# Attention probabilities divided by their sum on ScalarE before their transposes, instead of a division behind the value products

## The reference, cut to what matters

```python
def sink_probs(scores, mask, sinks):
    sc = jnp.where(mask, scores, NEG_INF)
    m = jnp.maximum(jnp.max(sc, axis=-1, keepdims=True), sink)
    p = jnp.exp(sc - m)
    denom = jnp.sum(p, axis=-1, keepdims=True) + jnp.exp(sink - m)
    return p / denom

def attn_prompt(q, k, v, sinks):   # blocks of 128 queries, each with its own and the previous 128 keys
    ...
    p = sink_probs(scores, mask, sinks)
    o = jnp.einsum("bnkgqs,bnskd->bnqkgd", p, vv)
```

## Time and profile before

| | |
|---|---|
| median of 3 runs | 907.57 us (906.25 to 912.13) |
| the profiled execution's own time | 907.48 us |
| its span in the profile | 905.5 us |
| mean granted TensorE clock | 0.996 |
| PE busy | 874.9 us, 97% of the span, 5635 instructions |
| PEld busy | 781.9 us (86%) |
| DVE busy | 558.0 us (62%) |
| ACT busy | 401.1 us (44%) |
| POOL busy | 253.1 us (28%) |

### The profile page before, as it was taken

How to read it: one execution, slowest core, us unless ns; L and a number is a source line. 1 busy time by engine, 2 the same in 40 slices (tenths; PEclk the granted TensorE clock), 3 DMA queues, 4 the chain that set the end, 5 groups by cost and what they waited for, 6 DMA issues and landing times. The chain is left out here.

```text
span 905.5 us, 16890 instructions
## 1 busy us (share of the span) xinstructions
PE 874.9 (97%) x5635; PEld 781.9 (86%) x5636; DVE 558.0 (62%) x1025; ACT 401.1 (44%) x732; POOL 253.1 (28%) x250
## 2 busy tenths in 40 slices
PE   8999999999999999999999999999799999999995
PEld 7777776878999999999999999999778888888884
DVE  5677775543489655665434955445887758487661
ACT  5666665311254443333211212223527757577562
POOL 2434332344231000000002540000152455364562
PEclk9999999999999999999999999999999999999998
DMA  8433331350532432223973138862549988989933
GB/s 281 140 96 115 127 76 36 99 215 1 193 97 74 147 107 96 95 96 110 335 282 90 65 91 285 303 222 93 170 135 312 338 269 292 335 247 315 299 43 60
DMA packets 79552, 153.55 MB, mean 170 GB/s; under 512 B 10701, under 2 KB 44173, under 8 KB 78960
## 3 DMA queue, kind: packets, MB, share of 16 engines
q1 hardware_dynamic: 72000, 134.84, 43.3%
q0 software_dynamic: 7488, 17.85, 8.6%
HBM read 122.80 MB, written 40.30 MB: 180 GB/s over the span
## 5 line engine op out<-in xcount | busy, mean ns | idle before, releaser
L1492 POOL TENSOR_TENSOR hT_lo_raw<-hT_lo_raw,arena 128x1056 f32<-128x1056 f32 x7 | 23.3, 3326 | 227.2 <-DVE arena L1738 227.2
L2486 DVE TENSOR_TENSOR hT_lo<-room,hT_hi (+1 forms) x32 | 72.2, 2292 | 17.2 <-ACT hT_hi L2175 17.2
L79 PE MATMUL psum<-w_hi,hT_hi 128*128 128x512 f32 (+3 forms) x216 | 79.1, 366 | 1.7 <-DVE hT_lo L1111 1.0
L79 PE MATMUL psum<-hT_hi,x_xT_hi 128*128 (+1 forms) x192 | 77.8, 405 | 1.4 <-DVE x_xT_lo L2638 0.7
L80 PE MATMUL psum<-hT_lo,x_xT_hi 128*128 (+1 forms) x192 | 75.7, 394 | 0.0
L81 PE MATMUL psum<-hT_hi,x_xT_lo 128*128 (+1 forms) x192 | 75.7, 394 | 0.0
L81 PE MATMUL psum<-w_hi,hT_lo 128*128 128x512 f32 (+3 forms) x216 | 75.3, 349 | 0.0
L80 PE MATMUL psum<-w_lo,hT_hi 128*128 128x512 f32 (+3 forms) x216 | 75.1, 348 | 0.0
L2115 POOL DMA_INDIRECT out_y<-y,put_at x23 | 46.1, 2005 | 91.1 <-DMA out_y<-y,put_at 67.8
L2175 ACT ACTIVATE hT_hi<-room (+1 forms) x32 | 59.9, 1922 | 11.5 <-PE psum L81 10.1
L1532 ACT ACTIVATE arena<-arena 128x264 f32<-128x264 f32 x64 | 26.9, 425 | 76.2 <-DVE arena L1727 75.6
(11 more groups left out here) (414 smaller groups left out, 2626.2 us busy)
## 6 DMA issues: line engine op xcount, KB each, us to landing
room<-in_w_gu SPq DMA_DIRECT2D x16, 2048.0 KB, 11.4
dn_raw<-in_w_dn SPq DMA_DIRECT2D x16, 1024.0 KB, 7.4
arena<-in_w_ab SPq DMA_DIRECT2D x24, 512.0 KB, 4.5
gate_rows<-arena SPq DMA_DIRECT2D x32, 264.0 KB, 2.4
arena<-gate_rows SPq DMA_DIRECT2D x16, 528.0 KB, 4.0
xT_chunk<-in_xT SPq DMA_DIRECT2D x8, 528.0 KB, 4.0
x_in<-in_x SPq DMA_DIRECT2D x8, 512.0 KB, 5.5
h_rows<-h_raw SPq DMA_DIRECT2D x8, 512.0 KB, 4.1
```

What stands on the lines that cost most here:

```text
L79: eng.matmul(out, lh, rh, start=first and k == 0, stop=False)
L1492: pool.tensor_tensor(here, here, part[v % 2], ALU.add).then_inc(h2_summed, 1)
L2486: dve.tensor_tensor(gu_lo[:, buf, ks], gu_raw[:, buf, ks], gu_hi[:, buf, ks].bitcast(F32), ALU.subtract).then_inc(gu_lo_made.sem, 1)
```

## The change

Each half's probabilities are now multiplied by the reciprocal of their own sum on ACT, in place, before they are transposed (`scale_probs`: four activations of 128x256 with a per-row scale). DVE inverts the sums half by half (`invert_dens(t, gp)`: two small operations). `dens_turn`, the spread to 128x512, `copy_rT` and `o_scale` are gone; `oa_high` and `oa_low` read bank 5 directly. Both copies of turned probabilities are DVE's. `oa_low` and the first inversion stand ahead of the second `mask_scores` on DVE; on ACT the first `probs` stands ahead of `copy_kv`, and the second `scale_probs` behind `h_high`. `mix(3)` goes between the two halves of `v_product(5)`. In the dense phase `low(4)` goes ahead of `weight_sum(0, "S4")`.

```diff
             def probs(t, gp):
                 if t >= 1:
-                    act.wait_ge(rd_made, t)
+                    act.wait_ge(rd_made, u - 1)
-            def copy_second_pT(t):
-                ...
-            def copy_rT(t):
-                ...
+            def scale_probs(t, gp):
+                k0 = block_keys(t)
+                act.wait_ge(rd_made, 2 * t + gp + 1)
+                for kv, i, j, g in heads_of(gp):
+                    ins = act.activation(p_sb[:, gp, j, k0:], p_sb[:, gp, j, k0:], ACT.Copy, scale=rden[:, gp, j:j + 1])
+                ins.then_inc(p_scaled, 1)
             def oa_high(t):
                 if t < PT:
-                    act.wait_ge(o_scaled, t + 1)
-                    src = o_n
+                    act.wait_ge(o_made, 2 * t + 2)
+                    src = bank(psum, 5)
 # ACT, step s = PT (the last)
                     probs(done, 0)
+                    scale_probs(done, 0)
+                    probs(done, 1)
                     copy_q(s)
-                    probs(done, 1)
+                    scale_probs(done, 1)
                     copy_kv(s)
-                    copy_second_pT(done)
                     vs_high(0)
-                    copy_rT(done)
 # ACT, steps s = 1 to 7
                     if s > 0:
+                        probs(done, 0)
                         copy_kv(s)
-                        probs(done, 0)
+                        scale_probs(done, 0)
                         probs(done, 1)
                     h_high(s + 1)
                     if s > 0:
-                        copy_second_pT(done)
+                        scale_probs(done, 1)
                     ...
                         copy_q(s)
                         copy_qT(s)
-                    if s > 0:
-                        copy_rT(done)
+                        oa_high(done)
 # PE
             def project_q(t, k0, k1):
-                if t >= 2:
-                    pe.wait_ge(rT_copied, t - 1)
             def probs_turn(t, gp):
-                pe.wait_ge(p_made, u + 1)
+                pe.wait_ge(p_scaled, u + 1)
             def values(t, gp):
                 if t >= 1:
-                    pe.wait_ge(o_scaled, t)
+                    pe.wait_ge(oa_lo_made, t)
-            def dens_turn(t):
-                ...
                 qk_turn(s)
-                dens_turn(s - 1)
             mix(2)
-            mix(3)
             for i in range(5, NT):
                 for half in range(2):
                     v_product(i, half)
+                    if i == 5 and half == 0:
+                        mix(3)
                 mix(i - 1)
 # DVE
-            def invert_dens(t):
-                ...
-            def o_scale(t):
-                ...
+            def invert_dens(t, gp):
+                dve.wait_ge(p_made, 2 * t + gp + 1)
+                step.did(dve.tensor_tensor(rden[:, gp, :], den[:, gp, :], sink_e[:, gp, :], ALU.add))
+                dve.reciprocal(rden[:, gp, :], rden[:, gp, :]).then_inc(rd_made, 1)
                 mask_scores(done, 0)
                 if s + 1 < NT:
                     h_scale(s + 1)
+                if done >= 1:
+                    oa_low(done - 1)
+                invert_dens(done, 0)
                 mask_scores(done, 1)
                 ...
                 copy_pT(done, 0)
+                invert_dens(done, 1)
                 ...
                     k_scale(s)
-                if done >= 1:
-                    oa_low(done - 1)
-                invert_dens(done)
+                copy_pT(done, 1)
                 ...
-                o_scale(done)
 # DVE, dense phase
             for piece in range(2):
                 fourth_sum(piece)
+            low(SLOTS - 1)
             weight_sum(0, "S4")
             dve.wait_ge(ob_lo, US)
             ...
-                low(g + SLOTS - 1)
+                if g > 0:
+                    low(g + SLOTS - 1)
```

More of the change, by code:

```diff
@@ L165, in attention_phase @@
         s_sb, p_sb = sp_sb[:, 0], sp_sb[:, 1:]
-        rT, o_n = (sp_sb[:, 0, 2 * n:2 * n + 2, :].rearrange("p g c -> p (g c)") for n in range(2))
         z, _ = brief((("z_qkv", [P, AW + KVW]), ("behind_z", [P, G * KV * HD])))
@@ L248, in attention_phase @@
         pT_made, pT_copied = sem("pT_made"), sem("pT_copied")
-        o_made, o_scaled = sem("o_made"), sem("o_scaled")
-        rd_made, rT_made, rT_copied = sem("rd_made"), sem("rT_made"), sem("rT_copied")
+        o_made, rd_made, p_scaled = sem("o_made"), sem("rd_made"), sem("p_scaled")
         oT_made, oa_hi_made, oa_lo_made = sem("oT_made"), sem("oa_hi_made"), sem("oa_lo_made")
@@ L639, in _ @@
                         copy_qT(s)
-                    if s > 0:
-                        copy_rT(done)
+                        oa_high(done)
                     if s + 3 < NT:
                         square(s + 3)
-                if s > 0:
+                if s == PT:
                     oa_high(done)
@@ L842, in sample_values @@
                 pe.wait_ge(v_cache_in, DMA)
-                pe.wait_ge(o_scaled, PT)
+                pe.wait_ge(oa_lo_made, PT)
                 d = slice(kv * HD, (kv + 1) * HD)
@@ L875, in sample_v_sum @@
                 pe.wait_ge(z_copied, 2 * NT)
-                pe.wait_ge(rT_copied, PT)
                 pe.matmul(bank(psum, 0)[0:NS, :], groups_sum, hs_parts, start=True, stop=True).then_inc(v_made, 1)
@@ L943, in _ @@
             values(PT - 1, 1)
-            dens_turn(PT - 1)
             qk_turn(PT)
@@ L1076, in copy_pT @@
                                 psum[:, 6 + first:8, :].rearrange("p a c -> p (a c)")).then_inc(pT_copied, 1)
-            def invert_dens(t):
[L1079 to L1086, removed]
-            def o_scale(t):
-                dve.wait_ge(o_made, 2 * t + 2)
-                dve.wait_ge(rT_copied, t + 1)
-                dve.tensor_tensor(o_n, bank(psum, 5), rT, ALU.mult).then_inc(o_scaled, 1)
+            def invert_dens(t, gp):
+                dve.wait_ge(p_made, 2 * t + gp + 1)
+                step.did(dve.tensor_tensor(rden[:, gp, :], den[:, gp, :], sink_e[:, gp, :], ALU.add))
+                dve.reciprocal(rden[:, gp, :], rden[:, gp, :]).then_inc(rd_made, 1)
             def oa_low(t):
                 dve.wait_ge(oa_hi_made, t + 1)
-                src = o_n if t < PT else bank(psum, 4)
+                src = bank(psum, 5 if t < PT else 4)
                 dve.tensor_tensor(oaT[1][:, :, toks(t)],
```

## The result

| | before | after |
|---|---|---|
| median of runs, us | 907.9 (906.25 to 913.83, 6 runs) | 931.34 (929.4 to 932.63, 6 runs) |
| ratio, 95% interval | | 1.0252 [1.0228, 1.0277] |
| profiled execution, own time / span, us | 907.48 / 905.5 | 932.39 / 930.4 |
| mean granted clock of TensorE | 0.996 | 0.989 |
| PE busy, share of the span | 97% | 94% |

The prediction was 924.4 (917 to 932): the sign, the place and the chain are as forecast, the sum is 7 us short. The page after opens with

A forecast was written before the change was run, and what follows sets the result against it. PE, busy 97% of the span, was taken to bound the kernel, so only its work or waits count. From 907.5, attention +19.2, `mix(3)` -1.7 and the gate -0.6 gave 924.4 us, range 917 to 932.

The forecast's parts named there:

- the second turn: Attention step, PE's transpose of the second half's probabilities: starts at 14.25 instead of 11.49 behind the scores, 2.75 us later.
- q's road: Attention, q's way through ACT and DVE from the second turn to the next scores: sets 5.07 us, unchanged.
- the second Exps: Attention step, ACT's Exps of the second half: start at 9.4 instead of 8.31, behind the later second mask.
- the stands: Attention step, PE's waits for ACT's scaling: 0.7 us before the first turn, about 2.05 before the second.
- The scaling: Attention, ACT's four passes for a half: 0.40 us apart and 0.49 for the last, 1.69 us in all.
- the cheap bound: Attention, scaling passes only 0.26 us apart, 1.2 us a half; the sum would be 3 to 4 us smaller.
- `h_high` in between: Attention, ACT's `h_high` moved between the second Exps and the second scaling: adds 1.05 us to the chain.
- `dens_turn` in the shade: Attention, PE's turn of denominators (0.4 to 0.6 us) stands in the shade of q's road; dropping it gives nothing back.
- Exclusion of GpSimd and DVE: Attention, `h_low` on GpSimd could delay the second inversion, holding the scaling 0.6 us in 6 steps: +3.6, upper end only.
- Step 8, mix, gate: Sample tile +0.9 us; `mix(3)` loses its whole wait, -1.7; the gate's wait moves to g = 5, -0.6.
- Attention: +19.2 us: Whole attention: 16.5 us for steps 1 to 6, 1.8 for step 7, 0.9 for step 8; uncertainty +-3.5.
- rival (d): Attention, PE's clock falls: 2.5 us behind each second turn at 1.2 GHz, 7 steps, 18 us more: 942; 6%.

The follow-up runs named there:

- measured with one: Changed kernel with only one head of four scaled in each half, division of the other three left out: 918.27 us, ratio 1.0116.
- the turns back: Changed kernel with the four transposes of the dropped denominators' turn put back on PE, result not read: 929.7 us, ratio 1.025.
- The two moves alone: Kernel before with only `mix(3)` between the halves of `v_product(5)` and `low(4)` ahead of the sum: 904.71 us, ratio 0.9975.
- the filled kernel: Changed kernel with 8 useless 128-column products on PE ahead of the second turn, steps 2 to 8: 926.81 us, ratio 1.0215.
- q's last part ahead: Changed kernel with the last part of q's projection ahead of the second turn instead of behind it: 919.39 us, ratio 1.013.
- the two filled kernels: Changed kernel with useless PE products ahead of the second turn: 32 of them, 959.09 us; 8 of them, 926.81 us.
- before with one turn of four: Kernel before with one of the four transposes of `dens_turn`, the other six heads' denominators not turned: 902.62 us, ratio 0.9952.

## Why the prediction was right, and where its sum was short

**What bounds it, and the chain.** Right. The scores follow the second turn through q's road and the turn follows DVE's and ACT's row of work. The second turn was forecast at 14.25 and is at 14.12; the second Exps 9.4 and 9.25; the stands 0.7 and 2.05, and 0.45 and 1.92. Five steps of 2.66 and step 7 with 1.7 make 15.0 us, where the forecast has 5 x 2.75 + 1.8 = 15.6; step 1 is 3.24 instead of 2.75, within the 1 us that its first inversion's wait was allowed. Together 18.2 against 18.3.

**The scaling.** Right: 1.69 us for four in the trace, and three of them are worth 1.20 in the chain where the chain was measured with one. The per-row Exp was the right neighbour, the cheap bound (0.26 us) was not.

**`h_high` in between.** 1.05 in the sum, which is its place in time; but taking it out gives only 0.5, for it covers the inversion's latency. A term of a chain is what stands there now, not what its removal returns.

**`dens_turn` in the shade.** Right: with the turns back the changed kernel's steps at full clock take the same time, with three of four away before's period changes by 0.04 us. The loss thus has no credit against it.

**Exclusion of GpSimd and DVE.** Kept for the upper end at 3.6 us; it did not occur. All sixteen adds of the inversion took 153 to 165 ns; in step 4 the second inversion ends at 97.74 and GpSimd's low part starts at 97.93.

**Step 8, mix, gate.** +0.7, -2.0 and -0.5 us, for +0.9, -1.7 and -0.6. The two moves alone gave 2.3 by the ratio.

**The clock.** This is the step that failed, and the mis-sized term of the sum: "Attention: +19.2 us" measured +26.4, and what is missing is the 7.5 us behind the second turns, which rival (d) described, come together with the forecast instead of in its place. The rival's price was too high in turn: it took the 2.5 us up to `values` at half speed and seven steps, 18 us; measured are 1.35 to 1.6 us in each of five steps. That the clock, and not a longer chain, makes this part is shown by the filled kernel: same waits on the same engines, 5.06 instead of 6.6 us behind the turn.

I held against rival (d) that gaps of 1.72 and 1.30 us had left the clock at full. The trace of before has a longer one that the prediction does not use: behind a stand of 1.99 us the granted clock falls, and the 32 products take 5.46 us. The changed kernel has the same stand at 665.36 and keeps the full clock there, with 3.84 us for the same products. The first fence is before, the second the changed kernel; the second row of each has length, PE busy and instructions, granted clock, DMA share, GB/s.

```profile
641.24 5.46 PE L2403 MATMUL psum<-ident 128*128 128x128 f32 x32 [1.99 <-POOL yT L2099]
642.00:644.00 2.00, 2.00 (x11) 0.50 0.96 291
```
```profile
665.36 3.84 PE L2373 MATMUL psum<-ident 128*128 128x128 f32 x32 [1.99 <-POOL yT L2069]
666.00:668.00 2.00, 2.00 (x20) 1.00 0.97 286
```

So a stand of 2 us could be known to lower the clock, though not that it would do so in most steps. (This fall cost the kernel before nothing: the work behind it waits for DVE, and starts at 648.21 and 672.33, 24.12 us apart, as the products themselves do.) What decides whether it falls stays open. It is not the stand's length alone: behind 1.92 us it fell in one step of the kernel with the turns back and held in the next; behind 1.32 us it fell in one step with q's last part ahead, and in step 8 with the scaling ahead of `h_high`. In step 1 the stand is 2.03 or 2.04 us: the clock held there in the changed kernel and fell in the two filled kernels and in the one with the turns back.

```profile
40.11 0.66 PE L776 MATMUL psum<-ident,sp_sb 128*128 128x128 f32 x4 [2.04 <-ACT sp_sb L571]
```

**The range.** It held by luck. Its upper bound of 932 rests on 3.6 us for an exclusion of GpSimd and DVE that never came and 3.5 us for steps that came within 0.1 us of the forecast; the clock, which did come, was priced at 942 and left outside. The lower bound of 917 does not follow from the terms that are given for it: 3.5 and 0.7 us below 924.4 are 920.

**A term that wasn't there.** The products of u lose 1.5 us, in two places: PE stands 0.43 us at 273.38, where before had no gap, and 0.99 us for `w_lo` at 286.20, where it had 0.35. By the order of the waits it seems to start further ahead, which is not shown: DVE waits for a load of the token rows, 2.96 us where it was 1.48.

```profile
266.99 1.26 DVE L1635 TENSOR_TENSOR arena<-arena,oaT_lo_raw 128x1056 f32<-128x1056 f32 x1 [2.96 <-DMA arena<-h_rows]
```

The load takes 9.1 us from issue to landing instead of 7.6. Every kernel with the changed attention shows it (8.7 to 9.2 us to landing), and so does before with one turn of four (8.8 us, DVE's wait 2.63); before and before with the two moves don't. I found no operation of the change that would cause it, and no experiment was made on it: its cause is open.

## What to carry to other kernels

Work on an engine that is half idle is not free: ACT was busy for 44% of the span, yet each pass put between the Exps and the turn reached PE in full, because ACT's idle time lay behind its waits. Before moving a small operation from the end of a chain to its middle, ask what it frees: here the normalisation left a place in the shade of q's road for one on the path of the probabilities. And when an edit makes TensorE stand in every pass of a loop, price the clock beside the stand: here it added 7.5 us to 18, and filling the stand with a few useless products of the right length brought 6.25 us of that back by the trace, 3.4 by the ratios of whole times. Look through the whole trace for falls of the clock before calling a stand harmless.

## What the runs showed of the hardware

The granted clock fell to its 1.2 GHz level behind stands of 1.92 us in five steps running and stayed there for about 3 us of dense work (0.53 and 0.62 in 80 to 84 us), although gaps of 1.72 and 1.30 us had not lowered it in the kernel before. The same loop with stands of 1.43 us, or with the stand filled, had the full clock in those steps. But equal stands went both ways: 1.99 us (fell before, held after), 2.03 and 2.04 us in step 1, 1.92 us with the turns back, and 1.32 us with q's last part ahead, where it fell in one step. With the turns back it fell once more at 205 us, behind three groups of small products, the widest of 64 columns, and with no wait of PE in front of it. The Trainium skill, TensorE: Matmul & The Clock Gate, section "A second HAM failure mode: psum-queue depth-cycling", tells of a kernel whose frequent short idles between groups of products made the clock go back and forth between its two levels, and this trace agrees in that: the granted clock went down and up again in each of steps 2 to 6. That it is their recurrence that counts is not shown, for in the kernel before a single place was enough.

A product of 128 columns with plain f32 operands shows as two entries and costs 0.23 us, 7.41 us for 32 of them back to back, where a turn of the same shape costs half of that (eight start and end within 1.09).
